# A decoder layer on one core: the low halves of three output weight tiles by adding DMAs, and the spatial products one tile later

## The chip, the cores and the metric

The kernel runs on one core of a Trainium2 chip. The metric is the device time of one execution in microseconds (us), the median of several runs; lower is better.

## What is computed

One layer of a decoder over 520 tokens (512 of a prompt, 8 single tokens of running sequences), all in float32:

```
x += 0.5 * SwiGLU_1(rms(x))
z  = rms(x) @ w_in + b_in            # columns [q | k | v | u | v_gate]
   A: sliding-window attention with sinks, 8 query heads on 2 key heads
   B: gelu(u) * (tril(W_s) v + b), v = layer_norm(gelu(v_gate)), chunks of 128
x += concat(A, B) @ w_out + b_out
x += 0.5 * SwiGLU_2(rms(x))
x += sigmoid(rms(x) @ w_ple_gate) * (p @ w_ple_proj)
y  = rms(x)
```

The outputs are y, the window buffers of keys and values, and the normalised rows of v of the last chunk (gm_v_prompt, 128 rows, and gm_v_sample, 8 rows).

## The kernel before, in words

Activations lie with features on the partitions: x is 8 tiles of 128 x 520. A float32 product is made of three products in a rounded format: each operand is split into a high half (`w_hi`, `xb_hi`, `mix_hi`: the rounded copy) and a low half (what rounding left), and TensorE adds high x high, high x low and low x high. So every weight tile of 128 output columns (128 x 1024 numbers) passes through three steps: SyncE loads it into `w_raw` by DMA, ScalarE writes the high half (`split_hi`, L711), and the low half is made in one of three ways: GpSimd subtracts (L1073), VectorE subtracts, or ScalarE writes the negated high half (L715) and GpSimd issues a DMA that adds the raw weights from DRAM onto it (L1068). The last way is used for the tiles named in `summed`. `w_lo` lies over `w_raw` in the same memory, so the raw tile is used up when its low half is written. Four slots are used in turn in the mixer stage, and a slot is loaded again when TensorE is done with its tile.

Between the two feed-forward stages lies the mixer. TensorE's program there is a list of steps, `mixer_steps()`: 14 input tiles ("gemm", u, k), each of 8 steps k of six matmuls of 260 columns (L1723), and then the output tiles ("out", m, k). Other stages are hung ahead of a step (u, k) by the table `extra`. Every engine walks the same list in the same order and takes from it what is its own, so the table sets the order on TensorE, VectorE, ScalarE and GpSimd at once. An engine waits only on semaphores, and everything behind a waiting instruction waits with it. The output tiles 0 and 1 are made together: steps 0 to 6 of both, then step 7 of both, since step 7 reads the last gated tile.

The stages near the end of the list, where the change lies:

- "p_turn" (7, r): TensorE turns the last probabilities, ScalarE copies them to `probs_t` (L964), and "values" 7 multiplies them with the value rows (L2044). "o_take" 7 splits the result, ScalarE (L971) and VectorE (L1492).
- "s_probs", "s_pt", "s_values", "s_take", "s_lo": the attention of the 8 single tokens. VectorE's `s_o` (L1596) ends it.
- "norm": VectorE centres and scales g (`g_rows`, L1516), and GpSimd makes the output rows `gv_rows` (L1143, L1145).
- "spatial" g: TensorE multiplies g with the chunk matrix (L2064; for g = 0 also the 8 tokens, L2061), VectorE adds gain and bias (L1534 to L1540).
- "gm" g: VectorE multiplies with gelu(u) (L1546), ScalarE makes the high half (L984); "gm_lo" g: VectorE makes the low half (L1550). These are the inputs of steps 4 to 7 of the output tiles.
- "evac" u: VectorE takes the finished input tile from the accumulators (L1430) and ScalarE adds the bias (L918, L920); "gelu_mid" (VectorE L1437, ScalarE L926) and "gelu_end" (VectorE L1445) finish the gelu of tile u.

In the kernel before, the high halves of output tiles 0, 1 and 2 are made ahead of steps (12, 4), (13, 4) and out (0, 4), and VectorE subtracts for the low halves (L1419) ahead of (12, 7), (13, 6) and out (0, 6).

## Time and profile before

| | us |
|---|---|
| median of 3 runs (985.79 to 986.68) | 986.0 |
| the profiled execution, its own time | 986.51 |
| its span, first to last instruction | 984.8 |
| TensorE busy in it | 963.6 |
| VectorE busy | 672.4 |
| ScalarE busy | 458.7 |
| GpSimd busy | 260.5 |

The profile is of one execution. Matmuls are pipelined, so their shown lengths overlap, and the distance from one start to the next tells what one costs. PE is TensorE, DVE VectorE, ACT ScalarE, POOL GpSimd. L numbers are lines of the kernel before; in the changed kernel the same lines stand a few numbers off.

### The profile page before, as it was taken

The page shows a single profiled execution, that of the slowest core. Times are in us where ns is not written, and L with a number is a line of the kernel's source. Part 1 is how long each engine was busy: PE and PEld are TensorE (multiplying, and loading weights), DVE is VectorE, ACT ScalarE, POOL GpSimd, SP SyncE. Part 2 cuts the span into 40 slices and gives each one's busy share as a digit, 9 for nine tenths or more (in the row PEclk, how much of TensorE's full clock was granted, in tenths as well). Part 3 has the DMA queues.
Part 4 walks back from the last instruction along what each step waited for, and adds up shares of the span by engine and source line. Part 5 has one row for each costly group of instructions (what it writes and reads, how often), then busy time and mean ns, then how long its engine had stood idle before and what let it go on. Part 6 is the DMA issues. An engine that isn't in the chain of part 4 may idle for free.

```text
span 984.8 us, 19296 instructions
## 1 busy us (share of the span) xinstructions
PE 963.6 (98%) x7949; PEld 947.1 (96%) x7949; DVE 672.4 (68%) x1063; ACT 458.7 (47%) x750; POOL 260.5 (26%) x150
## 2 busy tenths in 40 slices
PE   6999999999999999999999999999999999999997
PEld 4999999999999999999899999999999999999997
DVE  5899658856768654457775399857766758855576
ACT  6645425533435443566444455424543443545243
POOL 2302202211111226332318411301221211114521
PEclk9999999999999999999999999999999999999999
DMA  7962433252243336321114693253324325235202
GB/s 216 163 127 70 124 105 99 76 145 72 75 128 99 97 85 184 102 65 44 44 55 129 128 172 97 61 145 97 96 80 116 97 60 144 65 98 161 87 22 88
DMA packets 191603, 101.38 MB, mean 103 GB/s; under 512 B 12955, under 2 KB 189429, under 8 KB 191501
## 3 DMA queue, kind: packets, MB, share of 16 engines
q1 hardware_dynamic: 175904, 90.23, 32.2%
q0 software_dynamic: 11440, 5.77, 4.7%
q10 hardware_dynamic: 4172, 4.15, 1.4%
q8 instruction: 63, 1.03, 0.4%
q14 instruction: 24, 0.19, 0.1%
HBM read 97.59 MB, written 3.59 MB: 103 GB/s over the span
## 4 chain that ended last, share of the span: by engine, by line
PE 91%; DVE 5%; ACT 1%; DMA 1%; issue 1%; SPq 0%; DVEq 0%; ACTq 0%
PE ps L1723 49%; PE ps L1803 36%; PE ps L2141 2%; PE ps L1759 1%; DMA x_rows<-in_x_prompt_dram 1%; PE ps L2015 1%; PE ps L2044 1%; DVE w_lo L1327 0%; PE ps L1754 0%; DVE w_lo L1419 0%; PE ps L1748 0%; DVE xb_lo L1216 0%; DVE tt L1437 0%; DVE mix_lo L1550 0%; PE ps L2165 0%
## 5 line engine op out<-in xcount | busy, mean ns | idle before, releaser
L1803 PE MATMUL ps<-xo_hi,w_hi 128*128 128x260 f32 x1008 | 284.2, 282 | 0.7 <-DVE ab L1350 0.7
L1803 PE MATMUL ps<-xo_lo,w_hi 128*128 128x260 f32 x1008 | 284.7, 282 | 0.0
L1803 PE MATMUL ps<-xo_hi,w_lo 128*128 128x260 f32 x1008 | 284.4, 282 | 0.0
L1723 PE MATMUL ps<-h_hi,w_hi 128*128 128x260 f32 x960 | 195.8, 285 | 0.7 <-issue 0.6
L1723 PE MATMUL ps<-h_hi,w_lo 128*128 128x260 f32 x960 | 193.4, 283 | 0.0
L1723 PE MATMUL ps<-h_lo,w_hi 128*128 128x260 f32 x960 | 193.4, 283 | 0.0
L1803 PEld LDWEIGHTS ps<-xo_hi,w_hi 128*128 128x128 f32 x1008 | 189.6, 188 | 0.9 <-issue 0.9
L1803 PEld LDWEIGHTS ps<-xo_hi,w_lo 128*128 128x128 f32 x1008 | 189.8, 188 | 0.0
L1803 PEld LDWEIGHTS ps<-xo_lo,w_hi 128*128 128x128 f32 x1008 | 189.7, 188 | 0.0
L1723 PEld LDWEIGHTS ps<-h_hi,w_hi 128*128 128x128 f32 x960 | 148.1, 189 | 1.7 <-issue 1.2
L1723 PEld LDWEIGHTS ps<-h_lo,w_hi 128*128 128x128 f32 x960 | 148.8, 189 | 0.0
L1723 PEld LDWEIGHTS ps<-h_hi,w_lo 128*128 128x128 f32 x960 | 148.4, 189 | 0.0
L1094 POOL TENSOR_TENSOR w_lo<-w_a,w_hi 128x512 fp32r<-128x512 f32 x36 | 66.6, 1851 | 306.5 <-ACT w_hi L780 306.5
L1327 DVE TENSOR_TENSOR w_lo<-w_raw,w_hi 128x1024 fp32r<-128x1024 f32 x108 | 138.2, 1311 | 4.3 <-ACT w_hi L772 1.1
L790 ACT ACTIVATE snap<-ps 128x260 f32<-128x260 f32 x108 | 41.7, 386 | 170.8 <-PE ps L1803 157.9
L711 ACT ACTIVATE w_hi<-w_raw 128x1024 fp32r<-128x1024 f32 (+2 forms) x112 | 99.6, 898 | 41.2 <-DMA w_raw<-in_w_ffn_dram 35.6
L1073 POOL TENSOR_TENSOR w_lo<-w_raw,w_hi 128x1024 fp32r<-128x1024 f32 x30 | 73.8, 2467 | 103.7 <-ACT w_hi L711 103.7
L1232 DVE TENSOR_TENSOR w_lo<-w_raw,w_hi 128x768 fp32r<-128x768 f32 (+1 forms) x64 | 68.8, 1078 | 36.7 <-ACT w_hi L711 36.6
L1101 POOL TENSOR_TENSOR h_lo<-ab,h_hi 128x1040 fp32r<-128x1040 f32 x18 | 46.9, 2603 | 163.5 <-ACT h_hi L818 163.5
L1380 DVE SCALAR_TENSOR_TENSOR x<-ps,x 128x520 f32<-128x520 f32 x64 | 44.5, 695 | 64.0 <-PE ps L1723 63.9
L1723 PE MATMUL ps<-xb_hi,w_hi 128*128 128x260 f32 x304 | 65.7, 297 | 0.0
L1084 POOL TENSOR_TENSOR ssq<-ssq,sq 128x520 f32<-128x520 f32 x29 | 41.3, 1426 | 76.2 <-ACT sq L725 53.3
(276 smaller groups left out, 1476.5 us busy)
## 6 DMA issues: line engine op xcount, KB each, us to landing
w_raw<-in_w_ffn_dram SPq DMA_DIRECT2D x88, 256.0 KB, 3.0
w_a<-in_w_ffn_dram SPq DMA_DIRECT2D x36, 512.0 KB, 4.8
w_raw<-in_w_ffn_dram SPq DMA_DIRECT2D x48, 384.0 KB, 3.2
w_raw<-in_w_ffn_dram SPq DMA_DIRECT2D x16, 512.0 KB, 7.0
w_lo<-in_w_ffn_dram POOLq DMA_DIRECT2D x11, 512.0 KB, 8.4
w_raw<-in_w_in_dram SPq DMA_DIRECT2D x10, 512.0 KB, 4.0
w_raw<-in_w_ple_gate_dram SPq DMA_DIRECT2D x8, 512.0 KB, 3.6
x_rows<-in_x_prompt_dram SPq DMA_DIRECT2D x4, 512.0 KB, 5.7
```

The source lines that it names most:

```text
L711: nc.scalar.activation(w_at(wh, key), w_at(w_raw, key), ACT.Copy).then_inc(w_hi_ready, 1)
L790: nc.scalar.activation(snap[:, (1, 5, 6).index(r), :], ps[:, bank, 0:Q], ACT.Copy).then_inc(snapped, 1)
L1073: nc.gpsimd.tensor_tensor(w_at(wl, key), w_at(w_raw, key), w_at(wh, key).bitcast(F32), ALU.subtract).then_inc(w_lo_ready, 1)
L1084: nc.gpsimd.tensor_tensor(ssq[:], ssq[:], sq[:], ALU.add).then_inc(sq_added, 1)
L1094: nc.gpsimd.tensor_tensor(w_cells(wl, s, j, "a22"), w_a2[:, g % 2, 512:1024], w_cells(wh, s, j, "a22").bitcast(F32), ALU.subtract).then_in ...
L1101: nc.gpsimd.tensor_tensor(flat(h_lo[:, k:k + 2, :]), flat(abuf[:, p % 2, :, :]), flat(h_hi[:, k:k + 2, :]).bitcast(F32), ALU.subtract).the ...
L1232: nc.vector.tensor_tensor(w_at(wl, key), w_at(w_raw, key), w_at(wh, key).bitcast(F32), ALU.subtract).then_inc(down_lo, 1)
L1327: nc.vector.tensor_tensor(w_cells(wl, s, j, name, 2), w_cells(w_raw, s, j, name, 2), w_cells(wh, s, j, name, 2).bitcast(F32), ALU.subtract ...
L1380: nc.vector.scalar_tensor_tensor(out=halves(x[:, m, :]), in0=banks(*down_banks(c, m)), scalar=0.25, in1=halves(x[:, m, :]), op0=ALU.mult, ...
L1723: ins = pe.matmul(ps[:, bank + step * h, 0:HALF], w[:, c, w0:w0 + P], m_[:, sk, h * HALF:(h + 1) * HALF], start=(first and n == 0), stop=( ...
L1803: ins = pe.matmul(ps[:, b, 0:Q], w[:, c, k * P:(k + 1) * P], m_[:, op, k, :], start=(first and k == 0 and n == 0), stop=(k == 3 and n == 2 ...
L2141: ins = pe.matmul(ps[:, 2 * (m % 3) + h, 0:c1 - c0], w[:, c, w0:w0 + P], m_[:, k, c0:c1], start=(k == 0 and n == 0), stop=(k == KD - 1 and ...
```

## The change

Output tiles 0, 1 and 2 join `summed`: ScalarE negates their high halves, and GpSimd issues three adding DMAs for each (two of 64 x 4 x 128 numbers, one of 128 x 4 x 128, as the tile is laid out). The three subtractions on VectorE go. A new stage "out_w" m says where that is done: tiles 0 and 1 ahead of steps (12, 3) and (12, 4), and tile 2 ahead of (13, 4). Spatial product 0 moves from (12, 6) to (13, 0), product 1 from (13, 1) to (13, 2), "s_probs" from (12, 1) to (12, 2). GpSimd's work on the rows of g gets a stage of its own, "g_out", ahead of (12, 5), and the DMAs that write those rows out are issued by ScalarE at out (0, 6) and no more at the spatial products 2 and 3. The loads of the output tiles on SyncE stay as they are.

```diff
@@ mixer_steps: which stage stands ahead of which TensorE step
-        (12, 1): [("s_probs",)],
-        (12, 2): [("s_pt",), ("norm_rsqrt",)],
-        (12, 3): [("norm", 3), ("norm", 4), ("norm", 0), ("norm", 1), ("norm", 2)],
-        (12, 4): [("s_values",)],
-        (12, 6): [("s_take",), ("spatial", 0), ("gm", 0)],
-        (13, 0): [("gm_lo", 0), ("s_lo",)],
-        (13, 1): [("spatial", 1), ("gm", 1)],
-        (13, 3): [("gm_lo", 1)],
-        (13, 4): [("spatial", 2)],
+        (12, 2): [("s_probs",), ("s_pt",), ("norm_rsqrt",)],
+        (12, 3): [("out_w", 0), ("norm", 3), ("norm", 4), ("norm", 0), ("norm", 1), ("norm", 2)],
+        (12, 4): [("out_w", 1), ("s_values",)],
+        (12, 5): [("g_out", NB - 1), ("g_out", NB)],
+        (12, 6): [("s_take",)],
+        (13, 0): [("spatial", 0), ("gm", 0), ("s_lo",)],
+        (13, 2): [("gm_lo", 0), ("spatial", 1), ("gm", 1)],
+        (13, 4): [("out_w", 2), ("gm_lo", 1), ("spatial", 2)],
         (13, 6): [("gm", 2)],
         (13, 7): [("gm_lo", 2), ("spatial", 3)],
...
-        summed = [("up", 0, n) for n in range(2, N_STD)] + [("up", 1, n) for n in range(3, N_STD)]
-        first_out = [("out", m) for m in range(3)]
+        summed = ([("up", 0, n) for n in range(2, N_STD)] + [("out", m) for m in range(3)] +
+                  [("up", 1, n) for n in range(3, N_STD)])
+        parts = [NKV + 1 if key[0] == "out" else 1 for key in summed]
...
-            elif key in first_out:
-                eng.wait_ge(out_lo, first_out.index(key) + 1)
...
-                eng.wait_ge(lo_in[i % 2], 16 * (i // 2 + 1))
+                eng.wait_ge(lo_in[i % 2], 16 * sum(parts[i % 2:i + 1:2]))
...
+        def out_rows(m):
+
+            wo = a["w_out"][0][:, m * P:(m + 1) * P]
+            for c in range(NKV):
+                yield (slice(c * HD, (c + 1) * HD), slice(0, 4),
+                       wo[c * 256:(c + 1) * 256].rearrange("(j d) c -> d j c", d=HD))
+            yield slice(0, P), slice(4, 8), wo[512:1024].rearrange("(j d) c -> d j c", d=P)
+
...
@@ ScalarE
-                if kind == "gemm" and arg[1] == 4 and arg[0] > 0:
+                if kind == "gemm" and arg[1] == 4 and 0 < arg[0] < 12:
 
                     split_hi(mix_keys[arg[0] + 2])
-                elif kind == "out" and arg == [0, 4]:
-                    split_hi(("out", 2))
+                elif kind == "out_w":
+                    split_hi(("out", arg[0]))
...
-                elif kind == "spatial" and arg[0] >= 2:
-
-                    b = arg[0] - 2
-                    act.wait_ge(g_normed, b + 1)
-                    if b == 0:
-                        act.dma_start(o["gm_v_prompt"][0, 0], gv_rows[:, b, :]).then_inc(out_done, 16)
-                    else:
-                        act.dma_start(o["gm_v_sample"][0].rearrange("b t c -> (b t) c"), gv_rows[0:TS, b, :]
-                                      ).then_inc(out_done, 16)
+                elif kind == "out" and arg == [0, 6]:
+
+                    act.wait_ge(g_normed, 2)
+                    act.dma_start(o["gm_v_prompt"][0, 0], gv_rows[:, 0, :]).then_inc(out_done, 16)
+                    act.dma_start(o["gm_v_sample"][0].rearrange("b t c -> (b t) c"), gv_rows[0:TS, 1, :]
+                                  ).then_inc(out_done, 16)
...
@@ GpSimd
-                if key[0] == "down" or key in first_out:
+                if key[0] == "down":
                     return
                 if key in summed:
-                    _, s, n = key
                     i = summed.index(key)
                     pool.wait_ge(w_negated, i + 1)
                     if i > 1:
-                        pool.wait_ge(lo_in[i % 2], 16 * (i // 2))
+                        pool.wait_ge(lo_in[i % 2], 16 * sum(parts[i % 2:i:2]))
+                    if key[0] == "out":
+                        for rows_, ks, src in out_rows(key[1]):
+                            dst = w_at(wl, key).rearrange("p (k c) -> p k c", k=KD)[rows_, ks, :]
+                            pool.dma_start(dst, src, accum_op=ALU.add).then_inc(lo_in[i % 2], 16)
+                        return
+                    _, s, n = key
...
-                elif kind == "out" and arg == [0, 4]:
-                    split_lo(("out", 2))
-                elif kind == "norm" and arg[0] >= NB - 1:
+                elif kind == "out_w":
+                    split_lo(("out", arg[0]))
+                elif kind == "g_out":
...
@@ VectorE
-                if [kind, *arg] in (["gemm", 12, 7], ["gemm", 13, 6], ["out", 0, 6]):
-                    key = first_out[arg[0] - 12 if kind == "gemm" else 2]
-                    dve.wait_ge(w_hi_ready, index[key] + 1)
-                    nc.vector.tensor_tensor(w_at(wl, key), w_at(w_raw, key), w_at(wh, key).bitcast(F32),
-                                            ALU.subtract).then_inc(out_lo, 1)
-                elif kind == "stat_sum":
+                if kind == "stat_sum":
```

ScalarE's instructions from the tanh of input tile 11 to the high half of the single tokens' attention (`s_o`), before:

```order
L926 ACTIVATE tt<-tt 128x520 [waits gelu_arg]
L711 ACTIVATE w_hi<-w_raw 128x1024 [waits raw_in0]
L964 ACTIVATE probs_t<-ps 128x512 [waits probs_turned]
L994 ACTIVATE mix_hi<-s_o 64x4x8 [waits s_out]
L994 ACTIVATE mix_hi<-s_o 64x4x8
```

and after:

```order
L927 ACTIVATE tt<-tt 128x520 [waits gelu_arg]
L712 ACTIVATE w_hi<-w_raw 128x1024 [waits raw_in0]
L716 ACTIVATE w_lo<-w_hi 128x1024 [waits w_hi_ready]
L712 ACTIVATE w_hi<-w_raw 128x1024 [waits raw_in1]
L716 ACTIVATE w_lo<-w_hi 128x1024 [waits w_hi_ready]
L965 ACTIVATE probs_t<-ps 128x512 [waits probs_turned]
L992 ACTIVATE mix_hi<-s_o 64x4x8 [waits s_out]
L992 ACTIVATE mix_hi<-s_o 64x4x8
```

Between the tanh and the copy of the last turned probabilities (`probs_t`) stood one operation of 128 x 1024, and now stand four.

VectorE's instructions from the end of the single tokens' attention on, before:

```order
L1596 TENSOR_TENSOR s_o<-ps,s_pv 128x64 [waits s_p_taken,s_valued]
L1534 COPY s_sp<-ps 128x32 [waits bs_ready,spatial_made]
L1535 SCALAR_TENSOR_TENSOR sp<-ps,cols,bs_all 128x512 [waits dve_step]
L1540 TENSOR_SCALAR sp<-s_sp,cols,bs_all 128x8
L1546 TENSOR_TENSOR sp<-sp,gu 128x520 [waits gelu_done,spatial_taken]
L1419 TENSOR_TENSOR w_lo<-w_raw,w_hi 128x1024 [waits w_hi_ready]
L1430 TENSOR_TENSOR tt<-ps,rstd 128x520 [waits unit_done,z_done]
L1550 SCALAR_TENSOR_TENSOR mix_lo<-sp,mix_hi 128x520 [waits gm_hi]
L1602 TENSOR_TENSOR mix_lo<-s_o,mix_hi 64x4x8 [waits s_hi] x2
L1535 SCALAR_TENSOR_TENSOR diag<-ps,cols,bs_all 128x512 [waits bs_ready,stat_spread,spatial_made]
L1540 TENSOR_SCALAR diag<-s_sp,cols,bs_all 128x8
L1546 TENSOR_TENSOR diag<-diag,gu 128x520 [waits gelu_done,spatial_taken]
```

and after:

```order
L1594 TENSOR_TENSOR s_o<-ps,s_pv 128x64 [waits s_p_taken,s_valued]
L1428 TENSOR_TENSOR tt<-ps,rstd 128x520 [waits unit_done,z_done]
L1532 COPY s_sp<-ps 128x32 [waits bs_ready,spatial_made]
L1533 SCALAR_TENSOR_TENSOR sp<-ps,cols,bs_all 128x512 [waits dve_step]
L1538 TENSOR_SCALAR sp<-s_sp,cols,bs_all 128x8
L1544 TENSOR_TENSOR sp<-sp,gu 128x520 [waits gelu_done,spatial_taken]
L1600 TENSOR_TENSOR mix_lo<-s_o,mix_hi 64x4x8 [waits s_hi] x2
L1490 TENSOR_TENSOR mix_lo<-ps,mix_hi 128x256 [waits o_hi]
L1548 SCALAR_TENSOR_TENSOR mix_lo<-sp,mix_hi 128x520 [waits gm_hi]
L1533 SCALAR_TENSOR_TENSOR diag<-ps,cols,bs_all 128x512 [waits bs_ready,stat_spread,spatial_made]
L1538 TENSOR_SCALAR diag<-s_sp,cols,bs_all 128x8
L1544 TENSOR_TENSOR diag<-diag,gu 128x520 [waits gelu_done,spatial_taken]
```

The subtraction `w_lo` is gone, the taking of input tile 12 (`tt<-ps,rstd`) stands ahead of spatial product 0 and no more behind its gated tile, and the low half of the last attention values (`mix_lo<-ps,mix_hi`) stands ahead of the low half of that gated tile.

## Rows read from the trace of the kernel before

**Rows 1.** The page: span, and the busy time of TensorE.
```profile
span 984.8 us, 19296 instructions
...
PE 963.6 (98%) x7949; PEld 947.1 (96%) x7949; DVE 672.4 (68%) x1063; ACT 458.7 (47%) x750; POOL 260.5 (26%) x150
```

**Rows 2.** What TensorE waited for, 455 to 520 us: total us, times, longest.
```profile
PE ps L2061 <- DVE s_o L1596: 2.0, 1, 2.0
...
PE ps L1723 <- DVE mix_lo L1550: 1.0, 1, 1.0
```

**Rows 3.** TensorE's timeline: start us, us long, engine, line, operation.
```profile
486.67 0.40 PE L1723 MATMUL ps<-xb_hi,w_lo 128*128 128x260 f32 x2
489.02 1.02 PE L2061 MATMUL ps<-w_diag,g_rows 8*128 8x8 f32 x8 [1.96 <-DVE s_o L1596]
...
491.04 0.78 PE L1723 MATMUL ps<-xb_hi,w_hi 128*128 128x260 f32 x2
...
492.62 1.82 PE L2044 MATMUL ps<-probs_t,v_rows 128*64 128x128 f32 x16
494.37 0.51 PE L1723 MATMUL ps<-xb_hi,w_hi 128*128 128x260 f32 x2
...
513.49 0.40 PE L1723 MATMUL ps<-mix_hi,w_lo 128*128 128x260 f32 x2
514.87 0.50 PE L1723 MATMUL ps<-mix_hi,w_hi 128*128 128x260 f32 x2 [0.99 <-DVE mix_lo L1550]
```

**Rows 4.** Busy time by stretch, PEclk being the granted clock.
```profile
490.50:491.00 0.50, 0.50 (x6) 0.50 (x5) 0.00 (x0) 0.00 (x0) 0.50 (x1) 0.74 0.00 0
...
494.00:494.50 0.50, 0.50 (x7) 0.32 (x4) 0.50 (x2) 0.12 (x1) 0.00 (x0) 0.84 0.00 0
```

**Rows 5.** ScalarE's timeline of the same stretch.
```profile
485.89 0.64 ACT L926 ACTIVATE tt<-tt 128x520 f32<-128x520 f32 x1 [2.59 <-DVE tt L1437]
486.44 1.04 ACT L711 ACTIVATE w_hi<-w_raw 128x1024 fp32r<-128x1024 f32 x1
487.39 0.58 ACT L964 ACTIVATE probs_t<-ps 128x512 f32<-128x512 f32 x1
```

**Rows 6.** ScalarE's timeline in the first feed-forward stage.
```profile
24.51 1.07 ACT L715 ACTIVATE w_lo<-w_hi 128x1024 fp32r<-128x1024 f32 x1
25.48 1.04 ACT L711 ACTIVATE w_hi<-w_raw 128x1024 fp32r<-128x1024 f32 x1
26.55 1.06 ACT L715 ACTIVATE w_lo<-w_hi 128x1024 fp32r<-128x1024 f32 x1
```

**Rows 7.** VectorE's timeline, same columns.
```profile
491.42 0.19 DVE L1534 COPY s_sp<-ps 128x32 f32<-128x32 f32 x1 [2.55 <-PE ps L2064]
...
492.64 1.70 DVE L1546 TENSOR_TENSOR sp<-sp,gu 128x520 f32<-128x520 f32 x1
494.26 1.21 DVE L1419 TENSOR_TENSOR w_lo<-w_raw,w_hi 128x1024 fp32r<-128x1024 f32 x1
...
506.24 0.69 DVE L1430 TENSOR_TENSOR tt<-ps,rstd 128x520 f32<-128x520 f32 x1
508.42 0.70 DVE L1437 SCALAR_TENSOR_TENSOR tt<-tt 128x520 f32<-128x520 f32 x1 [1.49 <-ACT tt L920]
510.77 1.23 DVE L1419 TENSOR_TENSOR w_lo<-w_raw,w_hi 128x1024 fp32r<-128x1024 f32 x1 [1.66 <-ACT w_hi L711]
511.92 0.69 DVE L1445 SCALAR_TENSOR_TENSOR gu<-tt 128x520 f32<-128x520 f32 x1
```

**Rows 8.** VectorE's costliest group, 486 to 515 us.
```profile
L1419 DVE TENSOR_TENSOR w_lo<-w_raw,w_hi 128x1024 fp32r<-128x1024 f32 x3 | 3.7, 1220 | 1.7 <-ACT w_hi L711 1.7
```

**Rows 9.** GpSimd's timeline, last of the four operations on rows of g.
```profile
492.52 1.26 POOL L1145 TENSOR_TENSOR gv_rows<-gv_rows,lnb 8x512 f32<-8x512 f32 x1
```

**Rows 10.** Adding DMAs of GpSimd, 20 to 70 us: ns min, median, max; landing.
```profile
L1068 POOL DMA_DIRECT2D w_lo<-in_w_ffn_dram x6: 1542/1544/1699, 25.9 to 47.4; - x6
...
DMA to landing us min/median/max: 7.6/9.1/10.3
```

More of the change, by code:

```diff
@@ L478, in hybrid_decoder_layer @@
         gate_made, x_added = sem("gate_made"), sem("x_added")
-        w_negated, down_lo, out_lo = sem("w_negated"), sem("down_lo"), sem("out_lo")
+        w_negated, down_lo = sem("w_negated"), sem("down_lo")
         lo_in = [sem(f"lo_in{i}") for i in range(2)]
@@ L566, in hybrid_decoder_layer @@
         down_index = {key: i for i, key in enumerate(key for key in index if key[0] == "down")}
-        summed = [("up", 0, n) for n in range(2, N_STD)] + [("up", 1, n) for n in range(3, N_STD)]
-        first_out = [("out", m) for m in range(3)]
+        summed = ([("up", 0, n) for n in range(2, N_STD)] + [("out", m) for m in range(3)] +
+                  [("up", 1, n) for n in range(3, N_STD)])
+        parts = [NKV + 1 if key[0] == "out" else 1 for key in summed]
         late_gates = [("gate", m) for m in range(4, KD)]
         by_pool = {key: i for i, key in enumerate(key for key in index if key[0] != "down" and key not in summed
-                                                  and key not in first_out and key not in late_gates)}
+                                                  and key not in late_gates)}
         def lo_wait(eng, key):
@@ L665, in _ @@
                     load(key, w_dram["w_in"][:, :, c0:c0 + P])
-            wo = a["w_out"][0]
             for m in range(KD):
@@ L671, in _ @@
                 dst = w_at(w_raw, key).rearrange("p (k c) -> p k c", k=KD)
-                for c in range(NKV):
-                    sp_.dma_start(dst[c * HD:(c + 1) * HD, 0:4, :],
-                                  wo[c * 256:(c + 1) * 256, m * P:(m + 1) * P].rearrange("(j d) c -> d j c", d=HD)
-                                  ).then_inc(raw_in[slot[key]], 16)
-                sp_.dma_start(dst[:, 4:8, :], wo[512:1024, m * P:(m + 1) * P].rearrange("(j d) c -> d j c", d=P)
-                              ).then_inc(raw_in[slot[key]], 16)
+                for rows_, ks, src in out_rows(m):
+                    sp_.dma_start(dst[rows_, ks, :], src).then_inc(raw_in[slot[key]], 16)
             sp_.wait_ge(unit_done, done[("out", 0)])
@@ L1132, in _ @@
             for kind, *arg in steps:
-                if kind == "gemm" and arg[1] == 4 and arg[0] > 0:
+                if kind == "gemm" and arg[1] == 4 and 0 < arg[0] < 12:
                     split_lo(mix_keys[arg[0] + 2])
-                elif kind == "out" and arg == [0, 4]:
-                    split_lo(("out", 2))
-                elif kind == "norm" and arg[0] >= NB - 1:
+                elif kind == "out_w":
+                    split_lo(("out", arg[0]))
+                elif kind == "g_out":
                     b = arg[0]
```

## The prediction, made before the changed kernel was run

> **What bounds the kernel now.** The page first: TensorE is busy for 963.6 of 984.8 us [rows 1], so a change pays only where it takes away a wait of TensorE, or a time in which TensorE runs slowly. The profiled execution took 986.51 us, 1.7 more than its span and 0.5 more than the median of 986.0; I make the sum against the profiled one and carry the difference to the median. Then the list of waits, from the last quarter of the input tiles to the first output tile. TensorE waits there twice for more than half a microsecond: 2.0 us ahead of spatial product 0, put down to VectorE's `s_o`, and 1.0 us for the last low half `mix_lo`, ahead of step 7 of output tile 0 [rows 2]. TensorE's timeline places them: its work ends at about 486.9 and goes on at 489.02, and ends again at 513.7 and goes on at 514.87 [rows 3]. Behind the first wait the granted clock falls from full to half, 2.4 to 1.2 GHz: in the half microsecond from 490.5 the mean is 0.74, in the one from 494.0 it is 0.84, so it lay low from about 490.75 to 494.1 [rows 4]. The reader is to see it in the steps too: the six matmuls of (12, 6) took 491.04 to 492.62, 1.58 us, where a step takes 0.72 at the full clock (two matmuls each 0.24 us, as before 513.7). The second wait was followed by no fall.
>
> So the first place costs 2.1 us of standing and some 1.6 us of slow clock, and the second 1.15 us. Some 4.9 us is the most that this change can win, if nothing new appears.
>
> **What the change takes away.** (1) Three subtractions on VectorE, 3.7 us together, 1.22 each [rows 8]. All three lie between spatial product 0 and the last `mix_lo`, which VectorE is late with. The third also waited for its high half: from the middle of gelu 13 to its end VectorE needed 508.42 to 511.92, 3.50 us [rows 7], and without the high half and the subtraction there is the 0.70 us operation, ScalarE's tanh of 0.64 us [rows 5] and 0.1 us of hand-over, 1.45 us. (2) TensorE's wait for `s_o`, since spatial product 0 now stands behind "values" 7.
>
> **What it adds, and where that lands.** ScalarE walks in order. Between the tanh at 485.89 and the copy of the last turned probabilities stood one high half, and the copy began at 487.39 [rows 5]. Now four operations stand there. The first feed-forward stage shows this very sequence: a negation is followed by the next high half after 0.97 us, and a high half by its negation after 1.07 us [rows 6]. So four take 1.07 + 0.97 + 1.07 + 0.97 = 4.08 us, the copy begins at 486.44 + 4.08 = 490.5 and ends 0.58 us later, at 491.1. "values" 7 needs it. TensorE, with step (12, 6) moved ahead, is through at 486.9 + 0.7 = 487.6, and stands until 491.15: 3.5 us in place of 2.1. The wait for `s_o` is gone, and a longer one for `probs_t` has its place. "s_probs" one step later is worth at most 0.1 us and is left out. Moving the output DMAs of g costs nothing: they are two issues on ScalarE while it has no other work than the last gated tile.
>
> Then TensorE's way to spatial product 0. I take it that the clock falls as before and comes back at 494.1. "values" takes 492.62 to 494.37, 1.75 us, at the low clock, to 492.9; step (12, 7) 1.2 us at the low clock and 0.2 at the full one, to 494.3; spatial product 0 took 489.02 to 491.04 [rows 3], 0.15 us of it lost to the clock, so 1.87 us, to 496.2. VectorE began 0.38 us after its end (491.42 [rows 7]), so now at 496.55: 5.1 us later than before.
>
> **VectorE's chain from there.** Before, from 491.42 to TensorE's start at 514.87: 23.45 us. Out of it go two subtractions (2.4), 2.05 of the third place (3.50 less 1.45), the taking of input tile 12 (0.6), which now lies ahead of the chain, and 1.0 that the product with gelu(u) lost at 492.64: it took 1.70 us, and the next product of two such tiles, at 508.42, 0.70. Together 6.05 us. About 0.6 come back, since VectorE now waits for ScalarE's copy of the last attention values ahead of the first `mix_lo`. That leaves 18.0 us, and 514.55.
>
> The 1.0 us at 492.64 is the price of GpSimd. That product reads two tiles of SBUF, began while GpSimd was at its last addition on the rows of g (492.52 to 493.78 [rows 9]) and ended 0.56 us behind it [rows 7]. The Trainium skill, "SBUF — State Buffer", section "Who interferes with whom", says that a VectorE instruction with two inputs in SBUF and a GpSimd instruction that reads SBUF exclude each other, and that the one which issues first holds the port for its whole length. By that rule, the trace agrees.
>
> Where do GpSimd's four operations of 1.26 us, 5.0 us in all, lie now? They stand behind six adding DMAs. The two negations end at 488.6 and 490.6. The trace shows an issue for a whole tile alone, 1.54 us [rows 10]. If the cost goes with size, three issues take 1.54 us, the rows of g begin at 492.2 and end at 497.2, before VectorE comes to its first such product at 496.55 + 1.2 = 497.8: no loss. If each issue costs 1.54 us, three take 4.6, and the rows of g lie from 497.8 to 502.9, on the chain with all four: up to 3 us lost. I take the middle, 495 to 500, where two operations meet the chain: 0.8 to 1.7 us, 1.2 taken. The last `mix_lo` is then ready for TensorE at 515.75.
>
> TensorE itself gets there at 514.75: after (12, 7), from 495.2, it needed 18.55 us to 513.7, and now starts that way at 496.2. So it waits 1.0 us, and goes on at 515.75 against 514.87. **The sum is +0.9 us**: 987.4 for the profiled execution and 986.9 for the median.
>
> **The low halves' own deadlines.** Tile 0 is needed at 504.7, tile 1 at 509.7. With issues of 1.54 us the last DMA of tile 1 starts at 496.3 and lands, by the slowest landing of a whole tile, 10.3 us [rows 10], at 506.6. In time. Tile 2 is the tight one. ScalarE comes to it behind the tanh of tile 12, by my walk at 503.1, so the negation ends near 505.3. Needed is it two steps behind 515.75, at 517.2. With cheap issues and the median landing of 9.1 us it is there before 515.9; with issues of 1.54 us and 10.3 us at 518.7, 1.5 us late. Pieces of a quarter and a half tile should land sooner than a whole one, so I put nothing down. The Trainium skill, "DMA: Bandwidth & Descriptors", section "Anatomy of one DMA — SWDGE (gpsimd) path", gives 2.0 us plus the bytes at 436 GB/s. For a whole tile that would be 3.2 us, where the trace shows 7.6 at least, so the measurement decides and the adding costs more than the page's plain DMA; by the page alone tile 2 would be early by 5 us or more and the sum the same.
>
> **The rivals.**
> - *The clock stays low for longer* (slower). TensorE stands 3.5 us in place of 2.1. If it is then kept at 1.2 GHz until spatial product 0 is done, the rest of (12, 7) and the product cost some 1.8 us more, and the chain starts that much later: +2.7 us, 988.7. For it: the longer wait. Against it: before, TensorE worked without a gap at the low clock and had the full one back after 3.3 us. It decides above 1.1 us of extra loss. Chance 0.10.
> - *GpSimd lies on the chain with all its work, or tile 2 is late* (slower). Dear issues: 3 us lost to the port in place of 1.2, or 1.5 us of waiting ahead of output tile 2: +2.4 to +2.7 us, 988.6. For it: the only row of an issue is 1.54 us. Against it: these issues move a quarter or half as much. Chance 0.12.
> - *GpSimd is through in time.* The chain ends at 514.55, TensorE gets there at 514.75 without a wait: -0.1 us, 985.9. Chance 0.18.
> - *The clock doesn't fall this time, or for less.* 1.4 us are won at "values" and step (12, 7), TensorE arrives at 513.3 to 513.5: -0.5 with the port's loss to -1.5 without, 984.5 to 985.5. For it: the 1.0 us wait caused no fall. Against it: 2.0 us did. Chance 0.07.
> - *The three subtractions pay in full*, the copy of the probabilities being covered somehow: the first wait goes and the clock holds, -3 us or more, below 983.8. Against it speaks ScalarE's order, which I see no way around. Chance 0.03.
>
> The forecast as summed has the rest, 0.50, and its own range is 986.2 to 987.9.
>
> **How the numbers follow.** 0.2% is 2.0 us, about what a measurement of this kernel can tell from no change. Faster than that is the last rival and a little of the one before: 0.05. Slower, above 988.0, are most of the first two: 0.18. The rest is within: 0.77. The range takes in the two small gains and the two slower cases' centres: 984.8 to 988.7.
>
> **What would show it right or wrong.** ScalarE's last copy of `probs_t` begins near 490.5; TensorE waits 3.5 us there, put down to that copy, and no more for `s_o`; the granted clock lies at 0.50 for some 3 us behind it. VectorE takes spatial product 0 near 496.5, and one or two of its products over SBUF take 1.2 to 2 us in place of 0.7 beside GpSimd's `gv_rows`. TensorE waits about 1 us for the last `mix_lo`, and goes on near 515.8. The six later issues of GpSimd show their cost. Wrong would be: no wait for `probs_t`, a clock low for 5 us or more, or a wait for a DMA ahead of output tile 2.

## The result, and the profile after

The changed kernel took 989.2 us (median of 7 executions, 988.4 to 989.9), the kernel before 986.1 us on the same chip (7, 985.7 to 986.7): a ratio of 1.0031, with a 95% interval of 1.0021 to 1.0040. It is 3.1 us slower, where the sum said +0.9 and the range ended at 988.7. The profiled execution took 989.93 us.

The page, as in [rows 1]. TensorE's busy time rose by 4.3 us for the same 7949 matmuls, so it is slower work and not more work. Some 3.4 us of it are slow clock in the stretch looked at below; the other 0.9 arose far ahead of the change, in the first 30 us (65 matmuls between 20 and 30 us, against 72 before).

```profile
span 988.2 us, 19308 instructions
PE 967.9 (98%) x7949; PEld 951.0 (96%) x7949; DVE 670.3 (68%) x1060; ACT 462.0 (47%) x753; POOL 269.9 (27%) x159
```

What TensorE waited for, 478 to 522 us, answers to [rows 2]. The wait for `s_o` is gone, one for `probs_t` stands in its place, and the one for the last `mix_lo` is as long as before.

```profile
PE ps L2042 <- ACT probs_t L965: 1.8, 1, 1.8
PE ps L1721 <- DVE mix_lo L1548: 1.0, 1, 1.0
PE ps L2062 <- DVE diag L1538: 0.2, 1, 0.2
```

So the waits add up to the same 3 us, and the list alone would show no loss. ScalarE's timeline has the row of operations that was forecast, each at its forecast distance (compare [rows 5]): from the tanh's start to the copy's, 4.62 us.

```profile
486.84 0.64 ACT L927 ACTIVATE tt<-tt 128x520 f32<-128x520 f32 x1 [2.68 <-DVE tt L1435]
487.39 1.04 ACT L712 ACTIVATE w_hi<-w_raw 128x1024 fp32r<-128x1024 f32 x1
488.46 1.06 ACT L716 ACTIVATE w_lo<-w_hi 128x1024 fp32r<-128x1024 f32 x1
489.43 1.04 ACT L712 ACTIVATE w_hi<-w_raw 128x1024 fp32r<-128x1024 f32 x1
490.50 1.06 ACT L716 ACTIVATE w_lo<-w_hi 128x1024 fp32r<-128x1024 f32 x1
491.46 0.58 ACT L965 ACTIVATE probs_t<-ps 128x512 f32<-128x512 f32 x1
```

The tanh already starts 0.95 us later than in [rows 5]. That is the offset from the first 30 us and not the change; such an offset is nothing special: over the thirteen traces of this text, ScalarE's last `st<-st` (L960 here), which the change doesn't touch, starts at 480.3 to 482.3 us.

The busy time by stretches of 2 us, with the granted clock in the column behind POOL, shows what [rows 4] showed of before, and more of it. The clock is at half speed (1.2 GHz) from 486 to about 489.4, ahead of the wait, and again from about 492.9 to 499.7, behind it. Before, it was low for 3.3 us in this stretch.

```profile
486.00:488.00 2.00, 2.00 (x11) 2.00 (x12) 1.97 (x5) 1.16 (x2) 0.00 (x0) 0.50 0.00 0
488.00:490.00 2.00, 2.00 (x13) 2.00 (x12) 1.83 (x5) 1.97 (x3) 0.18 (x1) 0.64 0.00 0
490.00:492.00 2.00, 0.25 (x3) 0.04 (x1) 0.00 (x0) 1.97 (x4) 2.00 (x4) 1.00 0.24 30
492.00:494.00 2.00, 1.91 (x19) 1.57 (x20) 0.00 (x0) 0.44 (x3) 2.00 (x3) 0.71 0.83 101
494.00:496.00 2.00, 2.00 (x10) 1.77 (x10) 0.70 (x1) 0.16 (x1) 1.30 (x2) 0.50 1.24 156
496.00:498.00 2.00, 2.00 (x10) 1.98 (x11) 0.00 (x0) 1.18 (x2) 0.94 (x2) 0.50 0.99 140
498.00:500.00 2.00, 2.00 (x12) 2.00 (x12) 1.12 (x3) 0.00 (x0) 1.92 (x3) 0.58 1.09 245
```

TensorE's timeline answers to [rows 3]. The first slow stretch makes TensorE late for the wait, and that is why it stands only 1.85 us there. The second makes spatial product 0 (L2059, L2062) end at 498.5, and TensorE comes to step 7 of output tile 0 at 519.31 instead of 514.87.

```profile
489.85 0.40 PE L1721 MATMUL ps<-xb_hi,w_lo 128*128 128x260 f32 x2
492.10 1.30 PE L2042 MATMUL ps<-probs_t,v_rows 128*64 128x128 f32 x16 [1.85 <-ACT probs_t L965]
...
494.93 1.87 PE L2059 MATMUL ps<-w_diag,g_rows 8*128 8x8 f32 x8
496.73 2.08 PE L2062 MATMUL ps<-ws_t,g_rows 128*128 128x128 f32 x8
...
519.31 0.51 PE L1721 MATMUL ps<-mix_hi,w_hi 128*128 128x260 f32 x2 [1.02 <-DVE mix_lo L1548]
```

These are 4.4 us, the 0.95 us of offset included, of which 3.4 are left at the end. A wait of 0.7 us for VectorE (`ab`), which the second feed-forward stage had before, is not in the list of after; that accounts for most of the difference.

GpSimd's timeline: five issues of adding DMAs take 5.48 us, 1.1 us each on average, the sixth starts 1.76 us later and takes 1.31 us, and only then come the four operations on the rows of g, at 497.84 to 503.95.

```profile
489.82 5.48 POOL L1068 DMA_DIRECT2D w_lo<-in_w_out_dram  x5 [10.50 <-ACT w_lo L716]
497.06 1.31 POOL L1068 DMA_DIRECT2D w_lo<-in_w_out_dram  x1 [1.76 <-issue]
497.84 1.84 POOL L1146 TENSOR_TENSOR gv_rows<-g_rows,lng 128x512 f32<-128x512 f32 x1
499.76 1.28 POOL L1148 TENSOR_TENSOR gv_rows<-gv_rows,lnb 128x512 f32<-128x512 f32 x1
501.00 1.27 POOL L1146 TENSOR_TENSOR gv_rows<-g_rows,lng 8x512 f32<-8x512 f32 x1
502.34 1.61 POOL L1148 TENSOR_TENSOR gv_rows<-gv_rows,lnb 8x512 f32<-8x512 f32 x1
```

And VectorE beside it, as in [rows 7]. Three instructions of the chain are long: L1538 takes 1.33 us and a few rows further down, for the next group, 0.28; L1544 takes 1.72, where 0.70 is usual; the two of L1600 take 1.50, and 0.45 in a kernel where GpSimd is idle. That is 1.05 + 1.02 + 1.05 = 3.1 us.

```profile
498.84 0.19 DVE L1532 COPY s_sp<-ps 128x32 f32<-128x32 f32 x1 [3.04 <-PE ps L2062]
499.07 0.75 DVE L1533 SCALAR_TENSOR_TENSOR sp<-ps,cols,bs_all 128x512 f32<-128x512 f32 x1
499.73 1.33 DVE L1538 TENSOR_SCALAR sp<-s_sp,cols,bs_all 128x8 f32<-128x8 f32 x1
501.10 1.72 DVE L1544 TENSOR_TENSOR sp<-sp,gu 128x520 f32<-128x520 f32 x1
502.75 1.50 DVE L1600 TENSOR_TENSOR mix_lo<-s_o,mix_hi 64x32 fp32r<-64x32 f32 x2
...
505.89 0.28 DVE L1538 TENSOR_SCALAR diag<-s_sp,cols,bs_all 128x8 f32<-128x8 f32 x1
506.20 0.70 DVE L1544 TENSOR_TENSOR diag<-diag,gu 128x520 f32<-128x520 f32 x1
```

### The profile page after: what moved, and what is told of

The parts are those of the page before. It is cut to its first block, busy times and chain, and to the rows that moved or that the text cites. A ratio compares the mean times of both kernels' runs of the same rounds, so it can differ in the third digit from the quotient of the medians.

```text
span 988.2 us, 19308 instructions
## 1 busy us (share of the span) xinstructions
PE 967.9 (98%) x7949; PEld 951.0 (96%) x7949; DVE 670.3 (68%) x1060; ACT 462.0 (47%) x753; POOL 269.9 (27%) x159
## 4 chain that ended last, share of the span: by engine, by line
PE 93%; DVE 4%; ACT 2%; DMA 1%; issue 1%; SPq 0%; DVEq 0%; ACTq 0%
PE ps L1721 49%; PE ps L1801 37%; PE ps L2139 2%; PE ps L1757 1%; DMA x_rows<-in_x_prompt_dram 1%; PE ps L2042 1%; PE ps L2013 1%; PE ps L1752 0%; DVE xb_lo L1219 0%; ACT w_hi L712 0%; PE ps L1746 0%; PE ps L2163 0%; DVE sp L1544 0%; DVE h_lo L1219 0%; DVE p_lo L1616 0%
## 5 line engine op out<-in xcount | busy, mean ns | idle before, releaser
L1330 DVE TENSOR_TENSOR w_lo<-w_raw,w_hi 128x1024 fp32r<-128x1024 f32 x108 | 140.6, 1332 | 4.4 <-ACT w_hi L773 1.1
L1721 PE MATMUL ps<-xb_lo,w_hi 128*128 128x260 f32 x304 | 62.1, 286 | 0.0
```

What stands on the lines that cost most here:

```text
L1330: nc.vector.tensor_tensor(w_cells(wl, s, j, name, 2), w_cells(w_raw, s, j, name, 2), w_cells(wh, s, j, name, 2).bitcast(F32), ALU.subtract ...
L1721: ins = pe.matmul(ps[:, bank + step * h, 0:HALF], w[:, c, w0:w0 + P], m_[:, sk, h * HALF:(h + 1) * HALF], start=(first and n == 0), stop=( ...
```

## The experiments

The theory after the result: the four ScalarE operations ahead of the copy are the cause. They hold TensorE up, with a longer slow clock behind the wait, and the DMA issues behind them push GpSimd's rows of g onto VectorE's chain. The rivals were that the adding DMAs cost in themselves, that the later spatial product costs, and that the two losses are one. Ratios are to the kernel before, run on the same chip.

### 1. The high halves and negations of tiles 0 and 1 behind the copy

```diff
-        (12, 3): [("out_w", 0), ("norm", 3), ...
-        (12, 4): [("out_w", 1), ("s_values",)],
-        (12, 6): [("s_take",)],
+        (12, 3): [("norm", 3), ...
+        (12, 4): [("s_values",)],
+        (12, 6): [("out_w", 0), ("s_take",)],
+        (12, 7): [("out_w", 1)],
```

> The changed kernel, with the stages out_w 0 and 1 moved behind the copy of the last turned probabilities (ahead of steps (12, 6) and (12, 7)). Theory A (the four ScalarE operations ahead of the copy, and the slow clock behind the wait that they make, are the cost): TensorE doesn't wait for the copy, the clock holds, spatial product 0 is done some 5 to 7 us earlier: 981 to 983 us, clearly below the kernel before. Rival R1 (spatial product 0 stands a tile later and VectorE's chain starts late whatever ScalarE does): 988 to 989. Rival R2 (GpSimd's rows of g on VectorE's chain are the cost): they still follow the adding DMAs, so 986 to 988.

Measured: 982.4 us, ratio 0.9958 [0.9945, 0.9970]. The same work in another order is 6.8 us faster than the changed kernel and 4 us faster than before. The clock stays full from 486 on (4.00 of 4.00 us busy in each stretch), and no wait for `probs_t` is left:

```profile
486.00:490.00 4.00, 4.00 (x42) 3.56 (x40) 3.26 (x8) 3.64 (x7) 3.22 (x1) 1.00 0.00 0
490.00:494.00 4.00, 4.00 (x35) 3.98 (x35) 2.51 (x4) 3.26 (x4) 3.84 (x4) 1.00 0.46 132
```

What TensorE now waits for is the late DMA of tile 1, which GpSimd issued at 500.65:

```profile
PE ps L1722 <- DMA w_lo<-in_w_out_dram: 1.3, 1, 1.3
```

The edit moves more than ScalarE's operations. "g_out" at (12, 5) now stands ahead of the first issues, so GpSimd is through with the rows of g at 494.2, and VectorE loses only 0.9 us to them (L1539, 1.20 us). Rival R2's "they still follow the adding DMAs" was wrong, and this kernel alone can't tell the late copy from the rows of g:

```profile
486.78 3.50 POOL L1147 TENSOR_TENSOR gv_rows<-g_rows,lng 128x512 f32<-128x512 f32 x1 [8.03 <-DVE g_rows L1515]
...
492.96 1.27 POOL L1149 TENSOR_TENSOR gv_rows<-gv_rows,lnb 8x512 f32<-8x512 f32 x1
494.18 5.08 POOL L1069 DMA_DIRECT2D w_lo<-in_w_out_dram  x5
```

Kernel 9 can: it has the rows of g first too, but the four ScalarE operations still ahead of the copy, and took 987.5 us. So some 5.1 of the 6.8 us are ScalarE's order.

### 2. The changed kernel without the rows of g

GpSimd's four operations are left out and the gm_v outputs are zeros.

```diff
-                    nc.gpsimd.tensor_tensor(v, g_rows[0:n, b, :], lng[0:n, :], ALU.mult).then_inc(g_gained, 1)
-                    pool.wait_ge(g_gained, i + 1)
-                    nc.gpsimd.tensor_tensor(v, v, lnb[0:n, :], ALU.add).then_inc(g_normed, 1)
+                    nc.gpsimd.memset(v, 0.0).then_inc(g_normed, 1)
```

> The changed kernel without GpSimd's four operations on the rows of g: the output rows gm_v are filled with zeros by two short memsets. In the trace of the changed kernel three VectorE operations beside them were 3.1 us longer than their like. Rival R2 (the port is the cost): 3 us less, 986.2 us. Theory A: TensorE only waits 1.2 us there in all, so no more than that comes back: 988.0.

Measured: 988.0 us, 985.9 to 989.3, ratio 1.0013 [1.0003, 1.0022]. VectorE loses nothing to GpSimd any more, yet the median falls by 1.2 us only (1.8 by the two ratios). In the changed kernel TensorE waited just 1.2 us in all for VectorE's chain, 1.0 for `mix_lo` and 0.2 for `diag`; a shorter chain could give back no more than that in this execution. In the profiled execution TensorE waits 3.40 us for `probs_t` (3.5 had been forecast), and the clock is at half from 490 to 500:

```profile
488.00:490.00 2.00, 0.00 (x0) 0.00 (x0) 0.55 (x2) 1.97 (x3) 1.46 (x3) 0.95 0.00 0
490.00:492.00 2.00, 1.19 (x12) 1.19 (x14) 0.00 (x0) 1.16 (x4) 2.00 (x4) 0.50 0.72 87
...
498.00:500.00 2.00, 2.00 (x11) 2.00 (x11) 1.70 (x4) 0.00 (x0) 0.68 (x3) 0.50 0.84 133
500.00:502.00 2.00, 2.00 (x19) 2.00 (x19) 1.35 (x5) 0.91 (x2) 0.00 (x0) 0.99 0.51 62
```

### 3. The order of the changed kernel, but VectorE subtracts

The high halves stand where the change puts them; the negations and DMAs are gone, and the three subtractions are back in their places.

```diff
-        summed = ([("up", 0, n) for n in range(2, N_STD)] + [("out", m) for m in range(3)] + ...
+        summed = [("up", 0, n) for n in range(2, N_STD)] + [("up", 1, n) for n in range(3, N_STD)]
+        first_out = [("out", m) for m in range(3)]
...
```

> The changed kernel's order of stages, but with the low halves of output tiles 0 to 2 subtracted on VectorE again, ahead of (12, 7), (13, 6) and out (0, 6): no negations and no adding DMAs. Theory A: ScalarE has two operations of 1.05 us less ahead of the copy, so TensorE does not wait there for long and product 0 is 2 to 3 us earlier; VectorE has 3.7 us more in its chain but nothing of GpSimd beside it: 987 to 988.5. Rival R1 (the later product is the cost): 989 or more, since VectorE's chain gets longer by the subtractions.

Measured: 983.7 us, ratio 0.9970 [0.9959, 0.9981]. Two operations ahead of the copy instead of four leave a wait of 1.2 us for it, the clock stays full behind it, and GpSimd, with no issues ahead of them, is through with the rows of g at 495.3, 8.7 us sooner than in the changed kernel. That is 3 us better than either expectation: the longer chain ends in a wait of 1.0 us for `mix_lo`, no longer than before, and there is no slow clock.

### 4 and 5. The clock held up by filling matmuls, with and without the rows of g

24 matmuls on data at hand are added ahead of "values" 7, their result unused. In the second kernel the rows of g are left out too.

```diff
+N_FILL = 24
...
+                    if i == 7:
+                        pe.wait_ge(z_scaled, 12)
+                        for _ in range(N_FILL):
+                            pe.matmul(ps[:, 0, 0:HALF], wh[:, cell[("in", 12)], 0:P], xb_hi[:, 0, 0:HALF],
+                                      start=True, stop=True)
                     pe.wait_ge(probs_taken, 2 * i + 2)
```

> The changed kernel with 24 more matmuls of 260 columns on TensorE ahead of the values product 7, written to a free accumulator that nobody reads: TensorE works through its wait for the copy. If the slow clock behind the wait is the larger part of the cost (theory A with the clock): the clock holds from the copy on, 3 us come back, 986 to 987. If it is the standing alone: no change, 989.2, or up to 1 more where the added matmuls outlast the wait.

Measured: 990.8 us, ratio 1.0045 [1.0032, 1.0059], so the filling makes it slower, which neither expectation had. It did what it should: the clock is full up to 506 us, the wait for the copy is 0.56 us, and VectorE starts its chain at 496.38, 2.5 us sooner. But GpSimd starts on the rows of g at 498.00 as in the changed kernel, so the chain now meets all of it and loses 5.2 us:

```profile
496.38 0.19 DVE L1533 COPY s_sp<-ps 128x32 f32<-128x32 f32 x1 [1.30 <-PE ps L2068]
496.61 0.75 DVE L1534 SCALAR_TENSOR_TENSOR sp<-ps,cols,bs_all 128x512 f32<-128x512 f32 x1
497.28 2.60 DVE L1539 TENSOR_SCALAR sp<-s_sp,cols,bs_all 128x8 f32<-128x8 f32 x1
499.91 0.70 DVE L1545 TENSOR_TENSOR sp<-sp,gu 128x520 f32<-128x520 f32 x1
500.53 2.52 DVE L1601 TENSOR_TENSOR mix_lo<-s_o,mix_hi 64x32 fp32r<-64x32 f32 x2
503.08 0.42 DVE L1491 TENSOR_TENSOR mix_lo<-ps,mix_hi 128x256 fp32r<-128x256 f32 x1
503.42 1.47 DVE L1549 SCALAR_TENSOR_TENSOR mix_lo<-sp,mix_hi 128x520 fp32r<-128x520 f32 x1
```

An instruction on 8 columns stands for 2.60 us and ends with GpSimd's first operation of 1.84 us (498.00 to 499.84). TensorE then waits 2.58 us for `diag` ahead of spatial product 3 (505.90), and behind that wait the clock falls: 0.78 from 506 to 508, 0.50 from 508 to 510 and 0.86 from 510 to 512, some 1.7 us lost.

> The changed kernel with both edits at once: the 24 filling matmuls ahead of the values product 7, and GpSimd's rows of g left out (gm_v is zeros). Alone, the fill made the changed kernel 1.6 us slower, and leaving the rows out made it 1.2 faster. If the slow clock and GpSimd's port hide each other (in the trace of the fill the clock held and product 0 was done 2.5 us earlier, but VectorE lost 5.2 us beside GpSimd): 985 to 986.5, some 4.4 less than with the fill alone. If the two costs are independent: 989.2 + 1.6 - 1.2 = 989.6.

Measured: 987.0 us, ratio 1.0005 [0.9996, 1.0015], 3.9 us less than with the rows of g. That lies just above the expected 985 to 986.5 and far from the 989.6 of independent costs. So the rows of g cost 3.9 us when the clock is full behind the copy (the 2.58 us of waiting and the later slow clock), and 1.2 in the medians when it isn't: the two losses hide each other. GpSimd's work is fixed in time by the issues, so a chain that starts late meets less of it, and TensorE, late by its own clock, waits less for the chain. Kernel 5 also shows what the late copy costs by itself: with the clock full and no rows of g it is still 4.5 us behind kernel 1. TensorE does nothing useful there for 3.6 us (in kernel 4 from 488.70 to 492.26).

### 6. The kernel before, with only the order of the spatial products and "s_probs" changed

```diff
...
-        (12, 6): [("s_take",), ("spatial", 0), ("gm", 0)],
-        (13, 0): [("gm_lo", 0), ("s_lo",)],
-        (13, 1): [("spatial", 1), ("gm", 1)],
...
+        (12, 6): [("s_take",)],
+        (13, 0): [("spatial", 0), ("gm", 0), ("s_lo",)],
+        (13, 2): [("gm_lo", 0), ("spatial", 1), ("gm", 1)],
...
```

> The kernel before with only the order of the spatial products, s_probs and s_take changed as in the changed kernel; high halves, subtractions on VectorE and GpSimd's rows of g stay where they were. Theory A (the later product is a gain, the adding DMAs at their place the loss): no wait for s_o and none for the copy, the clock holds: 982 to 983.5. Rival R1 (the later product is the loss): 987 or more.

Measured: 985.0 us, ratio 0.9989 [0.9981, 0.9998], between the two expectations: a small gain. The wait for `s_o` and the low clock are gone (0.3 us for the copy), but the gain comes back as a longer wait at the end of VectorE's chain, which still has its subtractions:

```profile
PE ps L1721 <- DVE mix_lo L1548: 2.8, 1, 2.8
```

### 7. As 1, with the spatial products in their old places

```diff
...
+        (12, 6): [("out_w", 0), ("s_take",), ("spatial", 0), ("gm", 0)],
+        (12, 7): [("out_w", 1)],
...
+        (13, 1): [("spatial", 1), ("gm", 1)],
...
```

> The changed kernel with out_w 0 and 1 behind the copy (as in e1) and the spatial products back at their old places, (12, 6), (13, 1) and (13, 4). If the later product is worth something by itself: TensorE waits 2 us for s_o again, and the clock may fall: 984.5 to 986. If only the place of the adding DMAs counts: the same as e1, 982.4.

Measured: 984.5 us, ratio 0.9982 [0.9974, 0.9991], 2.1 us more than 1. The 2.0 us wait for `s_o` is back, and behind it the clock is at 0.69 from 490 to 494. The later product is a gain here, not a cost.

### 8. As 1, with the low half of tile 0 subtracted by VectorE

Tiles 1 and 2 keep their adding DMAs; VectorE subtracts for tile 0 ahead of (12, 7), before its chain begins.

```diff
+        first_out = [("out", 0)]
...
+                if [kind, *arg] == ["gemm", 12, 7]:
+                    key = ("out", 0)
+                    dve.wait_ge(w_hi_ready, index[key] + 1)
+                    nc.vector.tensor_tensor(w_at(wl, key), w_at(w_raw, key), w_at(wh, key).bitcast(F32),
+                                            ALU.subtract).then_inc(out_lo, 1)
...
```

> e1 with the low half of output tile 0 subtracted by VectorE ahead of (12, 7), where VectorE is idle, and only tiles 1 and 2 by adding DMAs. In e1 TensorE waited 1.3 us for the last adding DMA of tile 1, which GpSimd issued as the sixth. With three issues less ahead of it: no wait there, 1.0 to 1.3 us less than e1, 981.2. If that wait was covering another (VectorE's last mix_lo): 0.3 us less at most.

Measured: 981.7 us, ratio 0.9958 [0.9945, 0.9972], the lowest median of all. The wait for tile 1's DMA (1.3 us) is gone, but a wait of 1.0 us for the last `mix_lo`, which kernel 1 didn't have, stands in its place. So the trace speaks for the second expectation, 0.3 us at most, and the ratio is the one of kernel 1; that kernel 8 is really faster than kernel 1 is not shown.

### 9. The rows of g ahead of the adding DMAs

```diff
-        (12, 3): [("out_w", 0), ("norm", 3), ("norm", 4), ...
+        (12, 3): [("norm", 3), ("norm", 4), ("g_out", NB - 1), ("g_out", NB), ("out_w", 0), ...
-        (12, 5): [("g_out", NB - 1), ("g_out", NB)],
```

> The changed kernel with the same work, but the rows of g stand on GpSimd ahead of the adding DMAs of output tile 0, as they stood ahead of that place before. Nothing else moves: ScalarE still has four operations ahead of the last copy of the probabilities. With the rows of g left out altogether the time fell by only 1.2 us of the 3.1 that VectorE had lost beside them. Theory (the port's loss and the slow clock hide each other): GpSimd does the rows of g from about 487 to 494, ahead of VectorE's chain, which loses nothing; TensorE's wait for the copy and the low clock stay; about 988.0 us, 987.4 to 988.6. Rival (the two losses add up): 3.1 us less, 986.1. Second rival: the DMAs of tile 1, now issued five us later, come late and TensorE waits for them ahead of output tile 1: 989 or more.

Measured: 987.5 us, ratio 1.0013 [1.0000, 1.0027]. The median says little here: the twelve executions fall into groups by their mean granted clock.

| executions | mean granted clock | us |
|---|---|---|
| 5 | 0.996 to 0.998 | 985.3 to 985.7 |
| 1 | 0.997 | 986.9 |
| 4 | 0.993 or 0.994 | 988.1 to 988.8 |
| 2 | 0.994 | 990.6 and 991.1 |

The profiled one (988.78 us) is of the third line. TensorE waits 3.4 us for `probs_t`, VectorE's chain is free of GpSimd (L1537 takes 0.28 us, L1599 0.44), and the clock is at half from 491 to about 501:

```profile
490.00:492.00 2.00, 0.03 (x2) 0.03 (x2) 0.00 (x0) 1.97 (x4) 1.92 (x2) 0.73 0.00 0
492.00:494.00 2.00, 2.00 (x17) 1.67 (x17) 0.00 (x0) 0.31 (x2) 1.92 (x3) 0.50 0.04 8
...
500.00:502.00 2.00, 2.00 (x14) 2.00 (x14) 1.59 (x5) 0.67 (x2) 0.00 (x0) 0.71 1.37 188
```

So behind this wait the clock is low for some 10 us in some executions. In the others it must be low for a much shorter time: a mean of 0.998 leaves room for some 2 us of lost clock, 0.994 for 6. That is read from the means; no execution of the fast group was profiled. With the chain free the difference is 3.2 us (988.7 against 985.5, the middles of the two large groups). Kernel 2 shows the same two groups: three executions at 985.9 to 986.6 with a mean clock of 0.998, eight at 987.7 to 989.3 with 0.994 or 0.995. In the changed kernel the executions with a clock of 0.998 took 988.4, 988.5 and 989.0 us, those below it 989.2 to 989.9: only 1 us apart. By the argument of 5 that is because the loss beside GpSimd shrinks as the chain starts later; no pair of traces of this kernel shows it. Among the executions with a mean clock of 0.998, the rows of g cost 988.5 - 985.5 = 3.0 us by kernel 9, where they lie elsewhere, and 988.5 - 986.5 = 2.0 us by kernel 2, where they are left out.

### 10. Only tile 1 behind the copy

```diff
-        (12, 4): [("out_w", 1), ("s_values",)],
+        (12, 4): [("s_values",)],
+        (12, 7): [("out_w", 1)],
```

> The changed kernel with only the high half and the negation of output tile 1 moved behind the last copy of the probabilities; those of tile 0 stay ahead of it. Theory (the place of ScalarE's operations costs only in so far as TensorE stands for the copy): the copy ends 2.0 us sooner, TensorE was standing for 1.85 us, so it no longer stands and the clock holds; the chain on VectorE starts some 6 us sooner, but GpSimd has three issues ahead of the rows of g, which then lie on the chain with all four operations (up to 3 us lost): 983.5 us, 983 to 984.5. Rival (each ScalarE operation ahead of the copy costs its own share): half of the 6.8 us that moving both brought, 985.8. Second rival (the clock falls anyway, for another reason than the wait): 987 or more, with a low clock and no wait in the profile.

Measured: 983.9 us, ratio 0.9979 [0.9970, 0.9988]: 5.4 us less than the changed kernel, four fifths of what moving both tiles gave. With two operations fewer the wait is 1.4 us, and the clock stays full:

```profile
490.00:492.00 2.00, 2.00 (x17) 1.82 (x15) 0.70 (x1) 1.67 (x3) 2.00 (x3) 1.00 0.75 89
```

So the cost goes by how long TensorE stands at the copy and whether the clock falls behind it, not by the number of operations ahead of it. (I had expected no stand at all, forgetting that TensorE here comes a microsecond sooner than in the changed kernel's slow stretch.) VectorE still loses 2.6 us beside GpSimd in it (L1545 takes 1.72 us, L1601 1.50). GpSimd has three issues in a row here and none is held up, so that is a second difference from the changed kernel.

### 11. The adding DMAs, with the spatial products in their old places

```diff
...
+        (12, 4): [("s_values",), ("out_w", 0)],
+        (12, 6): [("s_take",), ("spatial", 0), ("gm", 0)],
+        (13, 0): [("out_w", 1), ("gm_lo", 0), ("s_lo",)],
+        (13, 1): [("spatial", 1), ("gm", 1)],
...
+        (13, 4): [("out_w", 2), ("spatial", 2)],
```

The lines are those that differ from the changed kernel. Against the kernel before, the high halves of tiles 1 and 2 come earlier (they stood ahead of (13, 4) and out (0, 4)), and the rows of g are written out later.

> The kernel before in all its places, with one part of the change: the low halves of output tiles 0, 1 and 2 by negation and adding DMAs. Tile 0 ahead of (12, 4), as before, tile 1 ahead of (13, 0), tile 2 ahead of (13, 4), the rows of g ahead of the DMAs. Theory (the DMAs by themselves are a gain, small while TensorE's wait for the single tokens' attention stays): ScalarE has two operations ahead of the copy, which TensorE meets only after spatial product 0 and so without a wait; the 2.0 us wait for s_o and the low clock stay; VectorE's chain loses three subtractions and the last wait for mix_lo goes: 984.9 us, 984.5 to 985.5. Rival (the DMAs themselves are what costs): 987 or more, with a wait for a w_lo DMA or more time lost on VectorE beside GpSimd's issues. No effect: 986.1.

Measured: 984.3 us, ratio 0.9975 [0.9966, 0.9984]. Without the new order of the products the DMAs are a gain of some 1.6 us by the medians and 2.5 by the ratio; the last wait for `mix_lo` is gone, and no DMA is waited for.

## Why the prediction was wrong

**What held.** The row of four ScalarE operations, to a tenth of a microsecond (copy 4.62 us behind the tanh, 4.6 forecast); TensorE's wait for the copy in place of the one for `s_o` (3.5 us forecast; 3.4 in kernels 2 and 9, but 1.85 in the trace of after, where the slow clock had made TensorE late); no wait for `s_o`; no wait for tile 2's DMAs, which land 3.4 to 6.4 us behind their issue, sooner than whole tiles [rows 10]. The 1.0 us of waiting for the last `mix_lo` came out as forecast partly by luck: chain and TensorE were both some 2.6 us later than in the sum, the offset left out. The base of the sum held as well: kernel 9, in its executions with a mean clock of 0.998, took 985.5 us, and kernel 2 in its own 986.5; the rival "GpSimd is through in time" had 985.9.

**What failed: the port.** The step "I take the middle, 495 to 500, where two operations meet the chain: ... 1.2 taken" should have read 3.1. The rows of g began at 497.84, or 496.9 without this execution's offset, 1.9 us later than the middle. The cost of an issue was not to blame: three take 3.0 to 3.4 us in the traces, near the middle of my two bounds (1.54 and 4.6). The sixth in a row was held up for 1.8 us, which I had not considered; in kernels 1, 7 and 9 the trace puts this hold-up (1.4, 3.7 and 3.6 us) down to an earlier adding DMA, and kernels 8, 10 and 11, with three issues in a row, have none.

And I counted only VectorE's products of two whole tiles. The small operations stand just as long: L1538 on 8 columns and the two of L1600 on 64 x 32 make 2.1 of the 3.1 us. The rival with all of GpSimd's work on the chain had the right price, 988.6 against the 988.5 of the changed kernel's executions with a clock of 0.998, and a chance of 0.12; its reason, issues of 1.54 us, was not the one that came true.

L1600 reads two tiles of SBUF and so fell under the sentence that I had cited; I overlooked it. L1538 reads one tile and takes its other operands as scalars. The Trainium skill, "SBUF — State Buffer", section "Who interferes with whom", counts `tensor_scalar` among the operations that can enter a mode with both ports, if their operands meet its conditions, and says that the engine which comes second is then blocked for the whole instruction. By that sentence, the trace agrees: L1538 ends at 501.06 with GpSimd's second operation (501.04).

**What failed too: the clock.** "I take it that the clock falls as before and comes back at 494.1" fails in the trace of after, where it was low behind the wait for 6.8 us, and in most executions of kernel 2 and half of those of kernel 9. With the chain free it costs 3.2 us, near the 2.7 of the rival "the clock stays low for longer", which had 0.10. On top of the port it costs 1 us.

**Why both were missed.** I treated the two as separate small chances around a middle. Both come from where the stages "out_w" 0 and 1 stand: on ScalarE ahead of the copy, on GpSimd ahead of the rows of g. Kernel 9 takes away the second half only (989.2 to 987.5 us), kernel 1 both (982.4), and kernel 10, with one tile behind the copy, most of it (983.9). The order of the spatial products (6, 7) and the DMAs (11) are gains when they are had without it. That I saw no way around ScalarE's order, in the rival where the subtractions pay in full, was right for this change; kernel 1 is a way around it.

**What stays open.** Why the sixth issue in a row is held up (by 1.4 to 3.7 us in seven traces). Why the clock was already low from 486 us in the profiled execution of after, with TensorE busy ahead of it; no other trace here has that. And why the mean clock differs so much from one execution of a kernel to the next (kernels 2 and 9); that it comes back early in one and late in the other is the likely reading, but no trace of the fast group is there to show it.

## What to carry to other kernels

An operation put ahead of a copy that TensorE needs soon must be weighed with all that it holds up: here four operations of 1 us ahead of the copy, with their DMA issues ahead of the rows of g, made the kernel 3 us slower, and the same work behind both made it 4 us faster than before. Before a DMA is issued by GpSimd, ask what stands behind the issue on GpSimd, and which small VectorE operations run at the time when that work now falls. When two losses come from one cause, removing one of them alone may bring little (2) or even cost (4); try the cause.

## What was not expected of the hardware

- One kernel's executions lie 3 us apart (985.5 and 988.7 us, kernel 9) with mean granted clocks of 0.998 and 0.994; in the profiled one, of the slower group, the clock was at half for some 10 us behind a wait of 3.4 us. Waits of 1.0 to 1.4 us (kernels 8, 3, 1, 10) were followed by no fall and waits of 2.0 to 3.4 us (before, 2, 4, 7, 9, 11) by one; but one of 2.8 us in kernel 6, at 514.6, wasn't: the clock was 1.00 in each stretch up to 522.
- Three issues of adding DMAs in a row (two quarters and a half of a tile) took GpSimd 3.0 to 3.4 us, twice the 1.54 us of one issue for a whole tile [rows 10]. After five in a row the sixth was held up by 1.4 to 3.7 us.
- VectorE's operation on 128 x 8 numbers, 0.28 us alone, took 2.60 us (kernel 4) beside GpSimd's operations on the rows of g.
